# The opening of a two-block transformer kernel: products with the inverse root on GpSimd, pieces of three weight slabs on ScalarE, paired squares

## The chip, the cores and the metric

The kernel runs on one core of one Trainium2 chip. The time is the device time of one execution in microseconds: 2210.19 us before, the median of three runs (2209.67 to 2212.11).

## What is computed

Two transformer blocks on 512 tokens of width 1024, in float32. The first has a modulation (adaLN) from a vector c; the change lies in its first lines:

```
mod = silu(c) @ ada_w + ada_b
sh1, sc1, gt1, sh2, sc2, gt2 = split(mod, 6)
h = rms_norm(x, norm1_gain) * (1.0 + sc1) + sh1
z = h @ w_in            # then latent attention, sparse attention, output projections,
                        # a gated MLP; the second block has two layers more
```

where `rms_norm(x, g) = x * rsqrt(mean(x * x) + 1e-6) * g`.

## The kernel before

All activations lie feature-major: `xT` is 128 partitions x 8 chunks (k) x 512 tokens. For accuracy each operand of a matrix product is split into a high part (rounded) and a low part (the rest); every product of the input stage is three TensorE instructions (`three`, lines 1130 to 1132): high by high, high by low, low by high. Weights stream from memory as slabs of 128 x 2048 into the two buffers of `raw`; of each slab `w_hi` and `w_lo` are made, by GpSimd in this stage. A slab of `w_in` holds four chunks k; two slabs make one chunk of 512 output columns. Processing of one k is 12 TensorE instructions (four blocks of tokens by three). The first two slabs processed are numbers 2 and 3 of the stream (called first and second here), then numbers 0 and 1 (third and fourth), then the rest in order. The buffer of a slab is reloaded when its split is done (`slab_split`, waited for by SyncE, SP), and its `w_hi` and `w_lo` are free when TensorE is through with it (`slab_used`).

Each engine has one program in order; they meet through semaphores. The opening runs as follows.

- SP issues the transfers in the order c (`crow`), `xT`, `consts` (among them the mean matrix and the identity), `cols` (gains and biases as columns), then the rows of `ada_w` in pairs (shift and scale of chunk k; rows 0 to 2, a slab, 3 and 4, a slab, 5 to 7), then small tables.
- ScalarE computes silu(c) twice (L2154, L2155), waits for the whole of x, loads the table of Sqrt, and squares the eight chunks of x into `t1` (`norm`, L1991).
- TensorE multiplies each square by the mean matrix (L1144; a float32 product of 512 columns is two passes), then runs 16 products with the identity (L1149) that serve nothing but to keep it busy. ScalarE takes the root (L1998), VectorE the reciprocal into PSUM (L2969).
- VectorE computes the modulation: for each k two products of a row of `ada_w` with silu(c) summed into `mod` (`first_shift`, `first_scale`, L2924). ScalarE folds in biases and gain (`first_mod`, L2162, L2164).
- Then for each k: VectorE forms x times scale times inverse root in PSUM bank 5 (`first_part`, L2952), ScalarE adds the shift and rounds to `h_hi` (L2173), VectorE makes `h_lo` (`first_low`, L2957). With one bank for the part, the next part waits for the low half. Rows for k + 1 are computed between part and low half.
- GpSimd splits the first two slabs in pieces of 512 (`split_first`, high L789, low L786), later slabs whole or in pieces (`split`, L668, L672).
- TensorE waits for piece and low half of each k (`first_ready`) and starts; after the first two slabs (into banks 0 to 3) `chunk` does the next ones, a slab at a time, with other work between (`compress_turn`, 16 transposes, L1661, between the third and the fourth slab).

Of the kernel before, what the change touches and what calls it, by code (L numbers as in the profile page):

```python
# [28 lines left out]
KD = D_MODEL // P  # L29
# [192 lines left out]
def build(nc, xT_d, slabs_d, ada_d, c_d, cols_d, rows_d, consts_d, strips_d, pos_d, cpos_d,  # L222
# [5 lines left out]
    with ctx:  # L228
# [186 lines left out]
        const_loaded, crow_loaded, x_loaded = sem("const_loaded"), sem("crow_loaded"), sem("x_loaded")  # L415
        rest_loaded = sem("rest_loaded")
        ada_first_loaded = [sem(f"ada_first_loaded{q}") for q in range(KD)]
        mod_summed, mod_ready, inv_kept = sem("mod_summed"), sem("mod_ready"), sem("inv_kept")
# [144 lines left out]
        def _(sp):  # L563
# [18 lines left out]
            sp.dma_start(xT[:], xT_d).then_inc(x_loaded, 16)  # L582
            for dst, src in ((consts[:], consts_d), (cols[:], cols_d)):
                sp.dma_start(dst, src).then_inc(const_loaded, 16)
# [67 lines left out]
        def _(pool):  # L652
# [127 lines left out]
            def split_first(n):  # L780
                pool.wait_ge(slab_loaded[n], 16)
                cuts = [slice(a, a + PIECE) for a in range(0, SLAB, PIECE)]

                def low(j):
                    pool.wait_ge(piece_hi, 4 * n + j + 1)
                    nc.gpsimd.tensor_tensor(w_lo[:, n, cuts[j]], raw[:, n, cuts[j]], w_hi[:, n, cuts[j]].bitcast(f32),  # L786
                                            ALU.subtract).then_inc(piece_split, 1)
                for j in range(4):
                    nc.gpsimd.tensor_tensor(w_hi[:, n, cuts[j]], raw[:, n, cuts[j]], zero[:, 0:PIECE], ALU.add  # L789
                                            ).then_inc(piece_hi, 1)  # L790
                    if j > 0:
                        low(j - 1)
                pool.drain().then_inc(hi_done, 1)
                low(3)
                pool.drain().then_inc(slab_split, 1)
# [51 lines left out]
            split_first(0)  # L847
            split_first(1)
            with pool.Fori(1, N_IN // 2) as i:
                for s in (0, 1):  # L850
                    split(s, 2 * i + s, i, piece=PIECE)
# [273 lines left out]
        def _(pe):  # L1125
# [8 lines left out]
            def norm(t, residual=True, warm=16):  # L1134


                ks = (3, 5, 6, 7) if residual else range(KD)
                for k in ks:
                    if residual and k < 6:
                        pe.wait_ge(pair_ready, at_.pairs + 1)  # L1140
                        at_.pairs += 1
                    else:
                        pe.wait_ge(sq_ready, KD * at_.norms + k + 1)
                    last = nc.tensor.matmul(PS[:, 0, :], mean_w, t[:, k, :], start=not residual and k == 0,  # L1144
# [42 lines left out]
            def chunk(bank0, ready=None, banks_ready=None, between=None, n=512):  # L1187

                for s in (0, 1):
                    pe.wait_ge(slab_split, at_.slab + 1)  # L1190
                    slab_tokens(at_.slab % 2, h_hi, h_lo, 4 * s, 4, n, bank0, 1, s == 0, s == 1, ready,
# [461 lines left out]
            pe.wait_ge(const_loaded, 16 * 2)  # L1653
            norm(t1, residual=False)
# [137 lines left out]
            chunk(4, between=during_q)  # L1792
# [188 lines left out]
        def _(act):  # L1981
# [3 lines left out]
            def norm(t, hi, shift=None, residual=True):  # L1985

                A(small[:, 8:9], eps_c, ACT.Sqrt)
                for k in range(KD):
                    if residual:
                        act.wait_ge(x_ready, at_.x + k + 1)  # L1990
                    A(PS[:, k, :] if residual and k in (0, 2, 4) else t[:, k, :], xT[:, k, :], ACT.Square  # L1991
# [165 lines left out]
            act.wait_ge(x_loaded, 16)  # L2157
            norm(t1, None, residual=False)

            def first_mod(k):  # L2160
# [3 lines left out]
                A(mod[:, k:k + 1], mod[:, k:k + 1], ACT.Identity, bias=col("ada_b", k)).then_inc(mod_ready, 1)  # L2164

            for k in (0, 1, 2):
                first_mod(k)
            for k in range(KD):
                if k > 2:
                    first_mod(k)  # L2170
                act.wait_ge(part_ready, k + 1)
                act.drain()
                A(h_hi[:, k, :], PS[:, 5, :], ACT.Identity, bias=mod[:, k:k + 1]).then_inc(part_hi, 1)  # L2173
                if k == 2:
                    A(inv_rms[:], PS[:, 4, :], ACT.Copy).then_inc(inv_kept, 1)
# [477 lines left out]
        def _(dve):  # L2653
# [294 lines left out]
            def first_part(k):  # L2948
                dve.wait_ge(mod_ready, k + 1)
                if k > 0:  # L2950
                    dve.wait_ge(part_low, k)
                V.scalar_tensor_tensor(out=PS[:, 5, :], in0=xT[:, k, :], scalar=sc1[:, k:k + 1], in1=PS[:, 4, :],  # L2952
                                       op0=ALU.mult, op1=ALU.mult).then_inc(part_ready, 1)

            def first_low(k):
                dve.wait_ge(part_hi, k + 1)
                V.scalar_tensor_tensor(out=h_lo[:, k, :], in0=PS[:, 5, :], scalar=sh1[:, k:k + 1],  # L2957
                                       in1=h_hi[:, k, :].bitcast(f32), op0=ALU.add, op1=ALU.subtract
                                       ).then_inc(part_low, 1)

            dve.wait_ge(x_loaded, 16)
            dve.wait_ge(const_loaded, 16 * 2)
            then(V.scalar_tensor_tensor(out=norm1_b, in0=col("ada_b", KD, KD), scalar=1.0, in1=col("norm1", 0, KD),
                                        op0=ALU.add, op1=ALU.mult))
            for k in (0, 1, 2):
                first_shift(k)
                first_scale(k)
            dve.wait_ge(root_ready, 1)
            then(V.reciprocal(PS[:, 4, :], PS[:, 1, :]))  # L2969
            for k in (0, 1, 2):  # L2970
                first_part(k)
                if k == 1:
                    first_shift(3)
                elif k == 2:
                    first_scale(3)
                first_low(k)
            for k in range(3, KD):
                first_part(k)
                if k + 1 < KD:
# [730 lines left out]
```

## Time and profile before

| | |
|---|---|
| median of three runs | 2210.19 us |
| the profiled execution | 2209.41 us |
| span of that execution, first to last instruction | 2207.6 us |
| TensorE busy | 2147.7 us, 97% |
| VectorE busy | 1504.0 us, 68% |
| GpSimd busy | 1195.1 us, 54% |
| ScalarE busy | 954.0 us, 43% |

The chain that ended last lies on TensorE for 85% of the span and on VectorE for 8%. Shares of the span are means over stages with different limits. In the first of 40 slices of the span (55 us each) TensorE is busy for six tenths, in all the later ones but the last for nine tenths or more, so the opening is read by itself.

### The profile page before, as it was taken

What the parts mean: (1) busy time and instruction counts of PE and PEld (TensorE: products, weight loads), DVE (VectorE), ACT (ScalarE), POOL (GpSimd) and SP (SyncE); (2) the same over time, 40 slices, a digit from 0 to 9 for tenths busy, and PEclk for the clock granted to TensorE, in tenths of its full rate; (3) what the DMA queues carried; (4) which work ended last, traced back from release to release, by engine and by line L of the source; (5) the groups of instructions that cost most, each with busy time, mean ns of one, the idle gap of its engine ahead of it and who ended that gap; (6) DMA issues with size and microseconds to landing.
All of it is one profiled execution on the core that took longest, in us unless ns stands there. A gap on an engine that the chain in (4) does not pass through costs nothing.

```text
span 2207.6 us, 33182 instructions
## 1 busy us (share of the span) xinstructions
PE 2147.7 (97%) x12377; PEld 1839.9 (83%) x12377; DVE 1504.0 (68%) x2242; ACT 954.0 (43%) x1905; POOL 1195.1 (54%) x594
## 2 busy tenths in 40 slices
PE   6999999999999999999999999999999999999997
PEld 4788888877899988897887898888897887889886
DVE  6834777554666692897746776677996727767676
ACT  3264663011556610644743555412545725555312
POOL 4747403776477677745016644577653037544675
PEclk9999999999999999999999999999999999999999
DMA  8422202522133333232002222322221012223221
GB/s 318 156 72 83 68 30 94 189 80 96 58 116 115 113 140 134 77 115 77 1 13 84 96 96 95 115 96 85 106 85 69 1 35 82 88 103 115 96 96 57
DMA packets 32776, 206.78 MB, mean 94 GB/s; under 512 B 4080, under 2 KB 4336, under 8 KB 11632
## 3 DMA queue, kind: packets, MB, share of 16 engines
q1 hardware_dynamic: 32192, 200.27, 25.2%
q10 hardware_dynamic: 432, 4.46, 0.5%
q8 instruction: 99, 1.62, 0.3%
q14 instruction: 53, 0.43, 0.1%
HBM read 202.61 MB, written 2.10 MB: 93 GB/s over the span
## 4 chain that ended last, share of the span: by engine, by line
PE 85%; DVE 8%; issue 2%; ACT 2%; DVEq 1%; DMA 1%; POOL 1%; POOLq 0%; SPq 0%; ACTq 0%
PE PS L1130 18%; PE PS L1132 18%; PE PS L1131 18%; PE PS L1626 4%; PE PS L1615 4%; PE PS L1385 3%; PE PS L1387 3%; PE PS L1386 3%; PE PS L1461 2%; PE PS L1463 2%; PE PS L1462 2%; PE PS L1640 2%; PE PS L1260 1%; PE PS L1263 1%; PE PS L1262 1%
## 5 line engine op out<-in xcount | busy, mean ns | idle before, releaser
L668 POOL TENSOR_TENSOR w_hi<-raw,zero_c 128x512 fp32r<-128x512 f32 (+1 forms) x135 | 281.6, 2104 | 545.0 <-PE PS L1132 543.7
L672 POOL TENSOR_TENSOR w_lo<-raw,w_hi 128x512 fp32r<-128x512 f32 (+1 forms) x135 | 365.0, 2722 | 5.8
L1130 PE MATMUL PS<-b_hi,w_hi 128*128 128x512 f32 x512 | 203.1, 397 | 1.0 <-POOL w_lo L891 1.0
L1132 PE MATMUL PS<-b_hi,w_lo 128*128 128x512 f32 x512 | 203.0, 396 | 0.0
L1131 PE MATMUL PS<-b_lo,w_hi 128*128 128x512 f32 x512 | 203.0, 396 | 0.0
L3376 DVE TENSOR_TENSOR b_lo<-a_all,b_hi 128x512 fp32r<-128x512 f32 x44 | 162.6, 3734 | 49.3 <-ACT b_hi L2511 49.3
L1130 PE MATMUL PS<-f_hi,w_hi 128*128 128x512 f32 x448 | 177.6, 396 | 0.7 <-DVE f_lo L2668 0.7
L1132 PE MATMUL PS<-f_hi,w_lo 128*128 128x512 f32 x448 | 177.6, 396 | 0.0
L1131 PE MATMUL PS<-f_lo,w_hi 128*128 128x512 f32 x448 | 177.6, 396 | 0.0
L691 POOL TENSOR_TENSOR w_lo<-raw,w_hi 128x512 fp32r<-128x512 f32 x48 | 71.1, 1481 | 92.7 <-ACT w_hi L2503 92.7
L1130 PEld LDWEIGHTS PS<-b_hi,w_hi 128*128 128x128 f32 x512 | 96.4, 188 | 24.7 <-POOL w_lo L891 1.2
L1132 PEld LDWEIGHTS PS<-b_hi,w_lo 128*128 128x128 f32 x512 | 96.4, 188 | 23.5
L1131 PEld LDWEIGHTS PS<-b_lo,w_hi 128*128 128x128 f32 x512 | 96.4, 188 | 23.5
L1626 PEld LDWEIGHTS PS<-z,ring 128*128 128x128 f32 x640 | 87.0, 191 | 25.7 <-issue 12.2
L1132 PEld LDWEIGHTS PS<-f_hi,w_lo 128*128 128x128 f32 x448 | 84.4, 188 | 20.5
L1130 PEld LDWEIGHTS PS<-f_hi,w_hi 128*128 128x128 f32 x448 | 84.4, 188 | 20.1 <-issue 1.0
L1131 PEld LDWEIGHTS PS<-f_lo,w_hi 128*128 128x128 f32 x448 | 84.4, 188 | 19.1
L2511 ACT ACTIVATE b_hi<-a_all 128x512 fp32r<-128x512 f32 x44 | 25.3, 623 | 171.4 <-PE PS L1132 171.4
L680 POOL TENSOR_TENSOR w_lo<-raw,w_hi 128x2048 fp32r<-128x2048 f32 (+1 forms) x18 | 59.1, 3295 | 62.3 <-ACT w_hi L2363 62.3
L776 POOL TENSOR_TENSOR w_lo<-raw,w_hi 128x512 fp32r<-128x512 f32 x54 | 70.8, 1311 | 38.0 <-ACT w_hi L2401 38.0
L3338 DVE SCALAR_TENSOR_TENSOR aux<-PS,cols,aux 128x511 f32<-128x511 f32 (+1 forms) x112 | 81.0, 741 | 14.7 <-ACT aux L2483 13.5
L1626 PE MATMUL PS<-z,ring 128*128 128x64 f32 x640 | 85.3, 266 | 1.3 <-ACT ring L2145 1.3
(600 smaller groups left out, 6890.1 us busy)
## 6 DMA issues: line engine op xcount, KB each, us to landing
raw<-slabs_dram SPq DMA_DIRECT2D x161, 1024.0 KB, 4.8
aux<-ada_dram SPq DMA_DIRECT2D x18, 512.0 KB, 5.5
ada_first<-ada_dram SPq DMA_DIRECT2D x11, 512.0 KB, 14.2
cmpw<-cmpw_dram ACTq DMA_DIRECT2D x2, 2048.0 KB, 12.0
ada_late<-ada_dram SPq DMA_DIRECT2D x8, 512.0 KB, 3.4
ada_last<-ada_dram SPq DMA_DIRECT2D x8, 512.0 KB, 6.1
xT<-xT_dram SPq DMA_DIRECT2D x1, 2048.0 KB, 9.2
out_dram<-t SPq DMA_DIRECT2D x4, 512.0 KB, 3.2
```

Of the source, the lines that this page charges most:

```text
L668: high = nc.gpsimd.tensor_tensor(w_hi[:, slot, c], raw[:, slot, c], zero[:, 0:c.stop - c.start], ALU.add)
L672: low = nc.gpsimd.tensor_tensor(w_lo[:, slot, c], raw[:, slot, c], w_hi[:, slot, c].bitcast(f32), ALU.subtract)
L691: return nc.gpsimd.tensor_tensor(pair_ring(w_lo, ct, n, what), pair_operand(ct, n, what), pair_ring(w_hi, ct, n, what).bitcast(f32), ALU.s ...
L776: nc.gpsimd.tensor_tensor(ring_slot(w_lo, j), operand(j), ring_slot(w_hi, j).bitcast(f32), ALU.subtract).then_inc(slab_split if name == "A ...
L1130: nc.tensor.matmul(out, a_hi_, b_hi_, start=start, stop=False)
L1131: nc.tensor.matmul(out, a_hi_, b_lo_, start=False, stop=False)
L1132: return nc.tensor.matmul(out, a_lo_, b_hi_, start=False, stop=stop)
L1385: nc.tensor.matmul(out, wh[:, k, :], xh, start=first, stop=False, skip_group_check=True)
L1615: last = nc.tensor.matmul(out, q, keys[:, 128 * lo:128 * (lo + nb)], start=True, stop=True)
L1626: last = nc.tensor.matmul(PS[:, 6 + m % O_BANKS, 64 * j:64 * j + 64], turned_slot(ring, v, 512)[:, 128 * b:128 * b + 128], jobs[m]["v"](lo ...
L3338: V.scalar_tensor_tensor(out=t[:, sh:], in0=src[:, 0:SEQ - sh], scalar=cols[:, w:w + 1], in1=t[:, sh:], op0=ALU.mult, op1=ALU.add)
L3376: V.tensor_tensor(b_lo[:, f, :], a_all[:, f, :], b_hi[:, f, :].bitcast(f32), ALU.subtract).then_inc(b_low_ready, 1)
```

## The change

x is loaded in two halves, each with its own semaphore, with the constants between them; the mean on TensorE waits for the constants only, and the columns are waited for together with the first modulation rows. ScalarE loads its table before it waits for x. VectorE adds the squares in pairs, so the mean is four products instead of eight, followed by 20 identity products instead of 16. The reciprocal goes straight into SBUF (`inv_rms`). GpSimd multiplies x by it, chunk by chunk, into `t1`, one chunk ahead. ScalarE makes `h_hi` from that with scale and shift, writes shift minus `h_hi` into PSUM (banks 4 and 5 in turn), and copies the pieces of the first three slabs into `w_hi`; GpSimd makes their `w_lo`. VectorE makes `h_lo` as product times scale plus what ScalarE left in PSUM. Rows 1 and 2 of the modulation come ahead of the first low half, rows 3 to 7 spread behind. The third slab is waited for by pieces on TensorE.

```diff
@@ -579,9 +579,11 @@
...
             sp.dma_start(crow[:], c_d.partition_broadcast(P)).then_inc(crow_loaded, 16)
-            sp.dma_start(xT[:], xT_d).then_inc(x_loaded, 16)
-            for dst, src in ((consts[:], consts_d), (cols[:], cols_d)):
-                sp.dma_start(dst, src).then_inc(const_loaded, 16)
+            for i in (0, 1):
+                sp.dma_start(xT[:, 4 * i:4 * i + 4, :], xT_d[:, 4 * i:4 * i + 4, :]).then_inc(x_loaded[i], 16)
+                if i == 0:
+                    sp.dma_start(consts[:], consts_d).then_inc(const_loaded, 16)
+            sp.dma_start(cols[:], cols_d).then_inc(ada_first_loaded[0], 16)
             for k in (0, 1, 2):
@@ -777,22 +779,24 @@
...
-            def split_first(n):
-                pool.wait_ge(slab_loaded[n], 16)
-                cuts = [slice(a, a + PIECE) for a in range(0, SLAB, PIECE)]
-
-                def low(j):
-                    pool.wait_ge(piece_hi, 4 * n + j + 1)
-                    nc.gpsimd.tensor_tensor(w_lo[:, n, cuts[j]], raw[:, n, cuts[j]], w_hi[:, n, cuts[j]].bitcast(f32),
+            def first_slabs():
+                def normed(k):
+                    nc.gpsimd.tensor_tensor(t1[:, k, :], xT[:, k, :], inv_rms[:], ALU.mult).then_inc(part_ready, 1)
+
+                pool.wait_ge(inv_kept, 1)
+                normed(0)
+                for k in range(KD + 4):
+                    if k + 1 < KD:
+                        normed(k + 1)
+                    n, c = k // 4 % 2, slice(PIECE * (k % 4), PIECE * (k % 4) + PIECE)
+                    if k >= KD:
+                        pool.wait_ge(slab_used, 1)
+                    pool.wait_ge(piece_hi, k + 1)
+                    nc.gpsimd.tensor_tensor(w_lo[:, n, c], raw[:, n, c], w_hi[:, n, c].bitcast(f32),
                                             ALU.subtract).then_inc(piece_split, 1)
-                for j in range(4):
-                    nc.gpsimd.tensor_tensor(w_hi[:, n, cuts[j]], raw[:, n, cuts[j]], zero[:, 0:PIECE], ALU.add
-                                            ).then_inc(piece_hi, 1)
-                    if j > 0:
-                        low(j - 1)
-                pool.drain().then_inc(hi_done, 1)
-                low(3)
-                pool.drain().then_inc(slab_split, 1)
+                    if k % 4 == 3:
+                        pool.drain().then_inc(hi_done, 1)
+                        pool.drain().then_inc(slab_split, 1)
@@ -844,9 +848,9 @@
...
             n_pieces = (N_IN + N_TAIL + N_QB + N_KVB) // 2
-            split_first(0)
-            split_first(1)
-            with pool.Fori(1, N_IN // 2) as i:
+            first_slabs()
+            split(1, 3, 1, piece=PIECE)
+            with pool.Fori(2, N_IN // 2) as i:
                 for s in (0, 1):
@@ -1134,14 +1138,14 @@
...
-                ks = (3, 5, 6, 7) if residual else range(KD)
+                ks = (3, 5, 6, 7) if residual else (1, 3, 5, 7)
                 for k in ks:
-                    if residual and k < 6:
+                    if not residual or k < 6:
                         pe.wait_ge(pair_ready, at_.pairs + 1)
...
                         pe.wait_ge(sq_ready, KD * at_.norms + k + 1)
-                    last = nc.tensor.matmul(PS[:, 0, :], mean_w, t[:, k, :], start=not residual and k == 0,
+                    last = nc.tensor.matmul(PS[:, 0, :], mean_w, t[:, k, :], start=not residual and k == ks[0],
                                             stop=k == ks[-1])
@@ -1187,8 +1191,9 @@
...
                 for s in (0, 1):
-                    pe.wait_ge(slab_split, at_.slab + 1)
-                    slab_tokens(at_.slab % 2, h_hi, h_lo, 4 * s, 4, n, bank0, 1, s == 0, s == 1, ready,
+                    if not ready or s:
+                        pe.wait_ge(slab_split, at_.slab + 1)
+                    slab_tokens(at_.slab % 2, h_hi, h_lo, 4 * s, 4, n, bank0, 1, s == 0, s == 1, None if s else ready,
                                 banks_ready if s == 0 else None,
@@ -1650,8 +1655,8 @@
...
             meet()
-            pe.wait_ge(const_loaded, 16 * 2)
-            norm(t1, residual=False)
+            pe.wait_ge(const_loaded, 16)
+            norm(t1, residual=False, warm=20)
@@ -1789,7 +1794,7 @@
...
             at_.slab += 2
-            chunk(4, between=during_q)
+            chunk(4, ready=lambda k: pe.wait_ge(piece_split, KD + k + 1), between=during_q)
             chunk(0, banks_ready=lambda tt: pe.wait_ge(cmp_dve if tt % 2 else cmp_act, tt // 2 + 1),
@@ -1988,6 +1993,8 @@
...
                         act.wait_ge(x_ready, at_.x + k + 1)
+                    else:
+                        act.wait_ge(x_loaded[k // 4], 16)
                     A(PS[:, k, :] if residual and k in (0, 2, 4) else t[:, k, :], xT[:, k, :], ACT.Square
@@ -2154,25 +2161,33 @@
...
             meet()
-            act.wait_ge(x_loaded, 16)
             norm(t1, None, residual=False)
...
                   bias=norm1_b[:, k:k + 1])
-                A(mod[:, k:k + 1], mod[:, k:k + 1], ACT.Identity, bias=col("ada_b", k)).then_inc(mod_ready, 1)
-
-            for k in (0, 1, 2):
+                A(mod[:, k:k + 1], mod[:, k:k + 1], ACT.Identity, bias=col("ada_b", k))
+
+            def piece_high(k):
+                n, c = k // 4, slice(PIECE * (k % 4), PIECE * (k % 4) + PIECE)
+                act.wait_ge(slab_loaded[n % 2], 16 * (n // 2) + 16)
+                A(w_hi[:, n % 2, c], raw[:, n % 2, c], ACT.Copy).then_inc(piece_hi, 1)
+
+            for k in range(KD):
                 first_mod(k)
-            for k in range(KD):
-                if k > 2:
-                    first_mod(k)
                 act.wait_ge(part_ready, k + 1)
                 act.drain()
-                A(h_hi[:, k, :], PS[:, 5, :], ACT.Identity, bias=mod[:, k:k + 1]).then_inc(part_hi, 1)
-                if k == 2:
-                    A(inv_rms[:], PS[:, 4, :], ACT.Copy).then_inc(inv_kept, 1)
+                A(h_hi[:, k, :], t1[:, k, :], ACT.Identity, scale=mod[:, KD + k:KD + k + 1], bias=mod[:, k:k + 1])
+                act.drain()
+                if k >= 2:
+                    act.wait_ge(part_low, k - 1)
+                A(PS[:, 4 + k % 2, :], h_hi[:, k, :].bitcast(f32), ACT.Identity, scale=-1.0, bias=mod[:, k:k + 1]
+                  ).then_inc(part_hi, 1)
+                piece_high(k)
+            act.wait_ge(slab_used, 1)
+            for k in range(KD, KD + 4):
+                piece_high(k)
             at_.part += KD
@@ -2945,40 +2960,26 @@
...
-            def first_part(k):
-                dve.wait_ge(mod_ready, k + 1)
-                if k > 0:
-                    dve.wait_ge(part_low, k)
-                V.scalar_tensor_tensor(out=PS[:, 5, :], in0=xT[:, k, :], scalar=sc1[:, k:k + 1], in1=PS[:, 4, :],
-                                       op0=ALU.mult, op1=ALU.mult).then_inc(part_ready, 1)
-
             def first_low(k):
                 dve.wait_ge(part_hi, k + 1)
-                V.scalar_tensor_tensor(out=h_lo[:, k, :], in0=PS[:, 5, :], scalar=sh1[:, k:k + 1],
-                                       in1=h_hi[:, k, :].bitcast(f32), op0=ALU.add, op1=ALU.subtract
-                                       ).then_inc(part_low, 1)
-
-            dve.wait_ge(x_loaded, 16)
-            dve.wait_ge(const_loaded, 16 * 2)
+                V.scalar_tensor_tensor(out=h_lo[:, k, :], in0=t1[:, k, :], scalar=sc1[:, k:k + 1],
+                                       in1=PS[:, 4 + k % 2, :], op0=ALU.mult, op1=ALU.add).then_inc(part_low, 1)
+
+            for k in range(0, KD, 2):
+                dve.wait_ge(sq_ready, k + 2)
+                V.tensor_tensor(t1[:, k + 1, :], t1[:, k, :], t1[:, k + 1, :], ALU.add).then_inc(pair_ready, 1)
+            dve.wait_ge(ada_first_loaded[0], 48)
             then(V.scalar_tensor_tensor(out=norm1_b, in0=col("ada_b", KD, KD), scalar=1.0, in1=col("norm1", 0, KD),
                                         op0=ALU.add, op1=ALU.mult))
-            for k in (0, 1, 2):
-                first_shift(k)
-                first_scale(k)
+            first_shift(0)
+            first_scale(0)
             dve.wait_ge(root_ready, 1)
-            then(V.reciprocal(PS[:, 4, :], PS[:, 1, :]))
-            for k in (0, 1, 2):
-                first_part(k)
-                if k == 1:
-                    first_shift(3)
-                elif k == 2:
-                    first_scale(3)
-                first_low(k)
-            for k in range(3, KD):
-                first_part(k)
-                if k + 1 < KD:
-                    first_shift(k + 1)
-                    first_scale(k + 1)
+            V.reciprocal(inv_rms[:], PS[:, 1, :]).then_inc(inv_kept, 1)
+            ahead = {0: (1, 2), 1: (3,), 3: (4,), 4: (5,), 5: (6,), 6: (7,)}
+            for k in range(KD):
+                for row_ in ahead.get(k, ()):
+                    first_shift(row_)
+                    first_scale(row_)
                 first_low(k)
```

## Rows read from the trace of the kernel before

**Rows 1.** Busy time by stage: stretch, length, busy of five engines, clock, DMA.
```profile
46.74:51.19 4.45, 3.05 (x13) 2.19 (x13) 3.82 (x7) 1.26 (x3) 4.45 (x4) 1.00 0.01 2
51.19:56.85 5.66, 5.66 (x24) 4.59 (x25) 4.25 (x20) 0.69 (x1) 0.53 (x1) 1.00 0.74 269
75.00:150.00 75.00, 75.00 (x362) 57.54 (x361) 50.88 (x63) 29.02 (x46) 43.95 (x35) 1.00 0.20 71
```

**Rows 2.** Chain that ended last, in order of time: start us, us, what.
```profile
1.20 9.21 DMA xT<-xT_dram
10.50 1.28 ACT L1987
...
12.66 9.85 PE PS L1144 x16
22.54 0.67 ACT PS L1998
23.23 3.37 DVE PS L2969
...
42.69 0.76 DVE PS L2952
43.45 1.12 DVEq L2946
...
45.85 0.76 DVE h_lo L2957
...
51.19 0.47 PE PS L1130
```

**Rows 3.** Timeline of the opening: start us, us, instruction, idle before and its releaser.
```profile
5.50 1.03 ACT L2154 ACTIVATE PS<-crow 128x1024 f32<-128x1024 f32 x1 [3.48 <-DMA crow<-c_dram]
6.46 1.04 ACT L2155 ACTIVATE crow<-crow 128x1024 f32<-128x1024 f32 x1
...
11.91 4.25 ACT L1991 ACTIVATE t<-xT 128x512 f32<-128x512 f32 x8
...
17.07 0.34 PEld L1144 LDWEIGHTS PS<-t,consts 128*128 128x128 f32 x1 [0.52 <-issue]
...
21.05 1.06 SPq L566 DMA_DIRECT2D ada_spare<-ada_dram  x1
...
22.34 7.07 PE L1149 MATMUL PS<-consts 128*128 128x256 f32 x32
...
37.74 0.39 ACT L2162 ACTIVATE mod<-mod,small,cols 128x1 f32<-128x1 f32 x1 [1.56 <-DVEq L2946]
```

**Rows 4.** DMA issues of the first 120 us: count, size, us to landing.
```profile
consts<-consts_dram SPq DMA_DIRECT2D x1, 460.0 KB, 9.6
```

**Rows 5.** The tile `ada_spare` (the last modulation rows), first 60 us.
```profile
DMA to landing us min/median/max: 16.6/18.2/19.0
```

**Rows 6.** Groups by line and shape, whole span: busy us, mean ns; idle before.
```profile
L811 POOL TENSOR_TENSOR m_rope<-q_m,trig 128x512 f32<-128x512 f32 x1 | 1.3, 1295 | 0.1
L786 POOL TENSOR_TENSOR w_lo<-raw,w_hi 128x512 fp32r<-128x512 f32 x8 | 10.3, 1285 | 0.4 <-issue 0.4
L2678 DVE RECIPROCAL t<-t 128x512 f32<-128x512 f32 x3 | 10.1, 3353 | 11.7 <-ACT t L2356 8.3 <-ACT t L1998 3.4
L2008 ACT ACTIVATE g_hi<-t,mod 128x512 fp32r<-128x512 f32 x8 | 5.7, 722 | 6.7 <-DVE t L2685 6.7
L2401 ACT ACTIVATE w_hi<-raw 128x512 fp32r<-128x512 f32 x54 | 34.0, 629 | 32.7 <-DMA raw<-slabs_dram 23.0 <-PE PS L1132 6.1 <-PE PS L1387 3.6
```

**Rows 7.** Timeline of GpSimd and VectorE behind the opening.
```profile
57.16 4.05 POOL L668 TENSOR_TENSOR w_hi<-raw,zero_c 128x512 fp32r<-128x512 f32 x4 [5.44 <-PE PS L1132]
61.29 5.03 POOL L672 TENSOR_TENSOR w_lo<-raw,w_hi 128x512 fp32r<-128x512 f32 x4
...
92.44 8.31 POOL L668 TENSOR_TENSOR w_hi<-raw,zero_c 128x512 fp32r<-128x512 f32 x4 [0.87 <-PE PS L1132]
93.16 2.47 DVE L2838 TENSOR_TENSOR z<-z,stats 128x2048 f32<-128x2048 f32 x1
```

More of the change, by code:

```diff
@@ L412, in build @@
         lam_c = small[:, 2:3]
-        const_loaded, crow_loaded, x_loaded = sem("const_loaded"), sem("crow_loaded"), sem("x_loaded")
+        const_loaded, crow_loaded, x_loaded = sem("const_loaded"), sem("crow_loaded"), [sem(f"x_loaded{i}") for i in (0, 1)]
         rest_loaded = sem("rest_loaded")
         ada_first_loaded = [sem(f"ada_first_loaded{q}") for q in range(KD)]
-        mod_summed, mod_ready, inv_kept = sem("mod_summed"), sem("mod_ready"), sem("inv_kept")
+        mod_summed, inv_kept = sem("mod_summed"), sem("inv_kept")
         piece_hi, piece_split = sem("piece_hi"), sem("piece_split")
@@ L3172, in _ @@
             meet()
-            dve.wait_ge(inv_kept, 1)
             scaled(t2, g_hi, g_lo, inv_rms[:], sc1, sh1)
```

## The prediction

> **What bounds the kernel now.** I read the busy time of the engines by stages first, then the chain of waits through the first 57 us, then the timeline of that stretch, and last the groups of instructions for prices. By stages TensorE is busy in every microsecond from 51.19 to 56.85 us and from 75 to 150, but between 46.74 and 51.19 in only 3.05 of 4.45 us [rows 1]. So TensorE is the limit once the opening is over, and a change in the opening is worth as many microseconds as it brings forward the moment from which TensorE no longer waits.
>
> The chain says what sets that moment [rows 2]. x lands at 10.41 us (1.20 + 9.21). ScalarE then loads its table (10.50, 1.28 us), the squares follow, the sixteen passes of the mean run from 12.66 to 22.51, the root takes 0.67, VectorE's reciprocal runs from 23.23 to 26.60. From there the chain stays on VectorE: part (0.76), two rows of the modulation with a drain (43.45 to 45.85, 2.40), low half (0.76), again and again, 4.0 us and more for one k. TensorE needs less: 24 products, two k, took 5.66 us, so 2.83 each [rows 1]. It therefore waits about a microsecond per k, and starts the seventh (k = 6) at 51.19 [rows 2]; from there it runs without a gap, and the first two slabs end at 56.85, with GpSimd, which waited for them, starting at 57.16 [rows 7]. Eight k are 22.6 us of work; 56.85 is the time to beat.
>
> **The change part by part.**
>
> *Constants and x.* x comes in two halves with the constants between, the columns after. The vector c has landed at 5.44, when ScalarE starts on it [rows 3], and x 5.0 us behind it. Taking the queue to deliver in order, the first half lands midway, at 7.9, the 460 KB of constants [rows 4], under a quarter of x, about 1.1 us later at 9.0, the second half at 11.5. The bytes ahead of the modulation's rows stay the same; the one more issue costs SP some 0.4 us, behind transfers that are queued anyway.
>
> *Squares.* ScalarE's table load no longer stands behind the wait for x. It follows the Silu that ends at 7.50 (6.46 + 1.04), so the first square starts at 7.55 + 1.41 = 8.96; the 1.41 is 11.91 less 10.50. Eight squares took 4.25, 0.53 each [rows 3]. Two are done at 10.1, four at 11.1; the second half runs from 11.55 to 13.8.
>
> *Pairs and mean.* VectorE adds four pairs at no more than the 0.76 of a part; it was idle until its first row. The first is done at 10.9, the last at 14.6. The mean is eight passes now, from 10.95. Before, the weight loads came 0.86 apart at 17.07 (0.34 + 0.52 idle [rows 3]); at that pace sixteen passes would take 13.8, and they took 9.85, so the later ones went at half of it, 0.43. Eight passes take 3.4 at the one pace and 6.9 at the other. I take the slow one nearly to the end, 17.7, since it still held at 17.07 last time. That is 4.8 before 22.51. Bounds of the mean's end: 16.5, if the last pass follows the last pair at once, and 17.9.
>
> *Root and reciprocal.* VectorE's modulation of row 0 takes 2.4 us from its landing near 15, so it is over before the root. Root 0.67 to 18.45, reciprocal into SBUF 3.35 [rows 6] to 21.9, against 26.60.
>
> *x times the root on GpSimd.* VectorE loses the part; GpSimd gains eight products and loses eight copies to the high half. The trace has the operation on that engine: a product of two SBUF tiles of 512 took 1.30, its low halves in the opening 1.29 [rows 6]. Bounds: 1.01, the copies (4.05 for four), and 2.08, the four that took 8.31 while VectorE worked on SBUF tiles alone [rows 7]. VectorE's rows and low halves here each read one SBUF tile and one of PSUM, as those beside the 1.29 did, so I take 1.30; GpSimd has 2.6 per k. The Trainium skill (GPSIMD Engine Reference, Engine selection) puts elementwise products on VectorE, GpSimd being about twice as slow for two inputs. The trace agrees, 1.30 against 0.76; by that rule alone the move loses 0.54 per k, by the rows it wins, because VectorE was the pace and GpSimd had room.
>
> *ScalarE per k.* Shift and scale 0.39 and no more than that again [rows 3], high half 0.72 [rows 6], the new negated copy to PSUM 0.67 as the root that writes there, the piece of the slab 0.63 [rows 6]: 2.7, and about 3.0 with the handovers. Bounds 2.7 and 3.6 (two drains at 0.2, a dearer high half with scale and bias).
>
> *VectorE per k.* Two rows and the drain 2.40, low half 0.76: 3.2 against 4.0. Rows 1 and 2 stand ahead of the first low half: reciprocal 21.9, rows to 27.0, low half 0 to 27.75, row 3 to 30.2, low half 1 to 30.95. No row is due at k = 2. Then every 3.2: low halves 3 to 6 at 34.9, 38.1, 41.3, 44.5. The last waits for ScalarE (row 7 done at 43.7, then the two small ones, high half and copy, 2.1, and 0.76): 46.6. Row 7 is wanted at 41.2; its last issue at 21.05 [rows 3] with the longest landing, 19.0 [rows 5], is 40.05.
>
> *TensorE.* Twenty identity products in place of sixteen: 32 instructions took 7.07 [rows 3], so 40 take 8.8, from 17.7 to 26.5, and it waits 1.3 us for k = 0 at 27.85. k = 1 starts at 31.05. From there every input is early (k = 5: 41.3 against 42.4; k = 6: 44.5 against 45.2; the slab's last low piece, GpSimd, 47.8 against 48.0), so seven k at 2.83 end at 50.9. **That is 5.95 us before 56.85.**
>
> *The third slab by pieces.* ScalarE copies its four pieces from 46.5 to 48.9, GpSimd's low pieces come at 49.2, 50.5, 51.8, 53.1; TensorE takes one per 2.83 from 50.9 and never waits. Late next is the fourth slab: its buffer comes free only with the last low piece, 47.9, it lands some 5 us later, at 53, or up to 56 if the compression weights, which ScalarE issues at 48.9, share the queue. GpSimd needs 9.2 for it (57.16 to 66.32 [rows 7]), so 62.3 to 65.2, and TensorE asks for it at 50.9 + 11.3 + 1.9 (the transposes) = 64.1. Loss 0 to 1.1; I take none. From the fifth slab on GpSimd waits for TensorE as before, and the lead stays.
>
> **Sum.** The profiled execution took 2209.41 for a span of 2207.6; less 5.9 that is 2203.5. The median, 2210.19, lies 0.8 above it, so I forecast 2204.3.
>
> **The rivals.**
>
> *Given back in part.* The hand-to-hand chain of ScalarE, GpSimd and VectorE has margins of only 0.2 to 1.1 us. At a pace of 3.4 per k from 27.85 TensorE ends at 27.85 + 7 x 3.4 + 2.83 = 54.5, a gain of 2.4; the fourth slab late by 1 to 2 us in its place leaves 4 to 5. For it: ScalarE takes on two more instructions per k. Against it: VectorE's 3.2 is measured work, and a k without a row gives slack. About 2207.2.
>
> *Slower: GpSimd becomes the bound.* Its sixteen instructions from 21.9 on now stand in front of TensorE. At a price p TensorE ends at 21.9 + 16p + 2.83, which passes 56.85 from p = 2.0. At the 2.08 of [rows 7] it ends at 58.0, 1.2 late; at 2.4 it is 63.1, 6.3 late, 2216.5. For it: GpSimd does slow down in company. Against it: 1.29 beside the very same rows. The Trainium skill (GPSIMD Engine Reference, Specifications) names VectorE instructions with two SBUF inputs as those that contend with GpSimd. By that rule only the four pair additions count, when GpSimd stands still; the trace agrees, 1.29 beside one SBUF input and 2.08 beside two.
>
> *No change at the end.* The opening gains 6 us and something that doesn't follow TensorE takes it back: 2209.5 to 2210.5. For it: 2150 us of program follow, and I have priced 15. Against it: loads are issued when slabs are split or used, so they move along, and TensorE is full from 75 to 150 us.
>
> **How the numbers follow.** Forecast 0.66 (its own range 2202.5 to 2205.8, from the mean's end at 16.5 or 17.9, and a microsecond lost to the fourth slab), given back in part 0.20, no change 0.08, slower 0.06. The range goes to 2201.8 below, for a pace that doubles early, and to 2208.3, which takes in most of the second case and leaves out the last two. A measurement of this kernel tells 0.2% (4.4 us) from no change: faster by that are the forecast and a little of the second case, 0.69; within it 0.26; slower 0.05.
>
> **What would show it.** In the new trace: first square near 9.0; mean over at 17.7 with eight passes; reciprocal ending at 21.9; products on GpSimd at 1.3; TensorE's first slab product near 27.9 and no wait from about 31; the two slabs over at 50.9; the fourth slab's low half before 64. A mean that ends after 19, a GpSimd product near 2, low halves more than 3.3 apart, or a wait of TensorE of over 2 us between 51 and 75 would make the prediction wrong.

## The result, and the profile after

The kernel after takes 2214.14 us, the median of 20 runs (2211.14 to 2215.78), beside 2210.84 for the kernel before, the median of 20 runs (2208.20 to 2213.63). The ratio is 1.0016, with a 95% interval of 1.0010 to 1.0022. It is 3.3 us slower. The forecast was 2204.3 in a range of 2201.8 to 2208.3, so both the sign and the range were wrong. The profiled execution after took 2213.46, for a span of 2211.3.

The head of the page of the kernel after, to be held against the busy times of before:

```profile
span 2211.3 us, 33193 instructions
...
PE 2150.0 (97%) x12377; PEld 1845.3 (83%) x12377; DVE 1501.1 (68%) x2238; ACT 966.5 (44%) x1924; POOL 1197.4 (54%) x590
```

TensorE is busy for 2.3 us more than before; where the time went has to be read from the opening. The timeline of the kernel after (start, length, instruction; in brackets the idle time before it and what ended it) gives the opening that [rows 2, 3] gave of before:

```profile
9.00 2.17 ACT L1998 ACTIVATE t<-xT 128x512 f32<-128x512 f32 x4
...
11.11 5.18 PE L1148 MATMUL PS<-t,consts 128*128 128x512 f32 x8 [11.11 <-DVE t L2970]
...
17.50 3.36 DVE L2977 RECIPROCAL inv_rms<-PS 128x512 f32<-128x512 f32 x1
...
21.01 2.51 POOL L784 TENSOR_TENSOR t<-xT,inv_rms 128x512 f32<-128x512 f32 x2 [20.17 <-DVE inv_rms L2977]
...
26.61 0.47 PE L1134 MATMUL PS<-w_hi,h_hi 128*128 128x512 f32 x1 [1.69 <-DVE h_lo L2965]
...
43.63 0.69 ACT L2185 ACTIVATE PS<-h_hi,mod 128x512 f32<-128x512 f32 x1
43.85 0.86 ACTq L2193 DMA_DIRECT2D cmpw<-cmpw_dram  x2
44.26 2.70 ACT L2175 ACTIVATE w_hi<-raw 128x512 fp32r<-128x512 f32 x5
49.65 1.88 ACT L2197 ACTIVATE z<-PS 128x2048 f32<-128x2048 f32 x1 [2.69 <-PE PS L1136]
...
62.70 5.58 POOL L674 TENSOR_TENSOR w_lo<-raw,w_hi 128x512 fp32r<-128x512 f32 x4
...
81.57 1.88 ACT L2197 ACTIVATE z<-PS 128x2048 f32<-128x2048 f32 x1 [18.81 <-PE PS L1136]
```

The same two takes of ScalarE (`z` from PSUM, after two slabs and after four) in the kernel before, with what ScalarE and its queue did ahead of them:

```profile
52.00 0.69 ACT L2173 ACTIVATE h_hi<-PS,mod 128x512 fp32r<-128x512 f32 x1 [1.20 <-DVE PS L2952]
52.01 0.86 ACTq L2178 DMA_DIRECT2D cmpw<-cmpw_dram  x2
57.05 1.88 ACT L2182 ACTIVATE z<-PS 128x2048 f32<-128x2048 f32 x1 [4.36 <-PE PS L1132]
...
81.19 1.88 ACT L2182 ACTIVATE z<-PS 128x2048 f32<-128x2048 f32 x1 [11.03 <-PE PS L1132]
```

The opening brought all that it was to bring and more. The first take came at 49.65 instead of 57.05, a lead of 7.40 us (6.4 against two other profiles of the old opening, see r2 and c1 below). The second came at 81.57 instead of 81.19. So 7.8 us were lost between the two takes. The chain of waits of the kernel after (start, length, what) shows where:

```profile
46.46 12.07 DMA raw<-slabs_dram
...
58.59 2.04 POOL w_hi L670 x2
```

This is the fourth slab. It was issued at 46.46 and took 12.07 us to land; in the kernel before it took 4.7. The waits of the kernel after in the first 170 us (engine, line, released by whom: total, times, longest):

```profile
POOL w_hi L670 <- DMA raw<-slabs_dram: 6.9, 1, 6.9
...
PE PS L1134 <- POOL w_lo L674: 5.8, 1, 5.8
...
PE PS L1134 <- DVE h_lo L2965: 1.7, 1, 1.7
```

and TensorE's first product of that slab in the timeline:

```profile
68.34 0.80 PE L1134 MATMUL PS<-w_hi,h_hi 128*128 128x512 f32 x1 [5.78 <-POOL w_lo L674]
```

GpSimd stood 6.9 us for the slab, split it until 68.3 (62.70 + 5.58), and TensorE stood 5.8 us for that. About half a microsecond of it is a slower split: 5.58 for the low half, where the kernel before took 5.03 [rows 7]. Then the clock came on top. By windows (stretch, length, busy time of PE, PEld, DVE, ACT and POOL, granted clock, DMA share, GB/s):

```profile
62.00:64.00 2.00, 0.56 (x6) 0.33 (x3) 1.73 (x3) 0.60 (x1) 1.92 (x3) 1.00 0.00 0
...
66.00:68.00 2.00, 0.00 (x0) 0.00 (x0) 2.00 (x2) 0.00 (x0) 2.00 (x2) 0.50 0.00 0
...
70.00:72.00 2.00, 2.00 (x6) 1.52 (x6) 2.00 (x2) 0.00 (x0) 2.00 (x3) 0.50 0.82 336
72.00:74.00 2.00, 2.00 (x10) 1.65 (x9) 1.83 (x3) 0.00 (x0) 1.92 (x2) 0.96 0.31 131
```

TensorE idled from 62.5 and the granted clock fell to 0.50, the 1.2 GHz level. Work came back at 68.3, the clock only at about 72.1 (a mean of 0.96 in 72 to 74): six products in 70 to 72, ten in 72 to 74. These 3.8 us at half speed cost 1.9. Wait and clock together are 5.8 + 1.9 = 7.7 of the 7.8.

Why was the slab late? The 4 MB of compression weights (two halves, `cmpw`) had been issued by ScalarE at 43.85, 2.6 us ahead of it. In the kernel before TensorE's first product of them is at 92.3, so they are in no hurry. There the fourth slab was issued at 41.32, and it had landed at 46.1, eleven microseconds before GpSimd came to it at 57.16 [rows 7]; the weights went out at 52.01. The change issues the slab five microseconds later and the weights eight earlier, so the two pass each other. The issue in the timeline of before, and the landings of the slabs issued there from 40 to 75 us:

```profile
41.32 0.33 SPq L570 DMA_DIRECT2D raw<-slabs_dram  x1
...
DMA to landing us min/median/max: 4.7/5.0/7.8
```

The 7.8 is the fifth slab, issued at 51.90 beside the weights; nothing waited for it.

The DMA queues of the kernel after show what the weights did to the slab (packets, MB, share of the 16 engines; q10 carries ScalarE's issues, q1 SP's). The first line is the stretch from 46.46 to 49.8, the other two that from 50 to 57:

```profile
q10 hardware_dynamic: 87, 1.43, 99.6%
...
q10 hardware_dynamic: 140, 2.03, 67.8%
q1 hardware_dynamic: 130, 1.00, 33.7%
```

For 3.3 us not one packet of the slab moved; where it is alone, in e5 below, its first packet starts 1.0 us after the issue. From then on the two queues moved nearly as many packets each, but those of the weights hold about twice the bytes, so the slab had a third of the traffic.

### The profile page after: what moved, and what is told of

Its sections match the earlier page's. It is cut to its first block, busy times and chain, and to the rows that moved or that the text cites. A ratio compares the mean times of both kernels' runs of the same rounds, so it can differ in the third digit from the quotient of the medians.

```text
span 2211.3 us, 33193 instructions
## 1 busy us (share of the span) xinstructions
PE 2150.0 (97%) x12377; PEld 1845.3 (83%) x12377; DVE 1501.1 (68%) x2238; ACT 966.5 (44%) x1924; POOL 1197.4 (54%) x590
## 4 chain that ended last, share of the span: by engine, by line
PE 81%; DVE 8%; DMA 2%; issue 2%; ACT 2%; DVEq 2%; POOL 2%; POOLq 1%; SPq 0%; ACTq 0%
PE PS L1134 17%; PE PS L1136 17%; PE PS L1135 17%; PE PS L1631 4%; PE PS L1620 4%; PE PS L1390 3%; PE PS L1392 3%; PE PS L1391 3%; PE PS L1645 2%; PE PS L1466 2%; PE PS L1468 2%; PE PS L1467 2%; DMA raw<-slabs_dram 2%; DVE PS L3464 1%; POOL w_lo L674 1%
## 5 line engine op out<-in xcount | busy, mean ns | idle before, releaser
L670 POOL TENSOR_TENSOR w_hi<-raw,zero_c 128x512 fp32r<-128x512 f32 (+1 forms) x131 | 275.8, 2123 | 543.8 <-PE PS L1136 536.8
```

The source lines that it names most:

```text
L670: high = nc.gpsimd.tensor_tensor(w_hi[:, slot, c], raw[:, slot, c], zero[:, 0:c.stop - c.start], ALU.add)
```

## The experiments

A reading used throughout is the lag: the start of one and the same ScalarE instruction in a run's trace less its start in the profiled execution of before, so that a negative number is a lead. Positions are those in the trace of before; from 160 on each is the median of a stretch.

| run | at 57 | at 81 | 160 to 225 | 245 to 300 | 750 to 800 | end |
|---|---|---|---|---|---|---|
| after | -7.40 | +0.38 | +0.41 | +1.43 | +3.10 | +3.77 |
| e1 weights later | -6.31 | -6.29 | -5.20 | -4.17 | -2.47 | -0.38 |
| e5 weights later still | -7.43 | -7.41 | -7.38 | -7.40 | -7.40 | -7.29 |
| q1 weights in order | -7.58 | -7.58 | -6.92 | -6.92 | -5.20 | -3.40 |
| w1 no idle TensorE | -6.26 | -1.02 | -1.00 | -0.98 | +0.77 | +2.52 |
| p1 e5 without pairs | -3.50 | -3.50 | -3.50 | -2.48 | +1.17 | +1.12 |
| b1 before, slab late | -0.85 | +8.89 | +8.91 | +8.90 | +10.68 | +10.60 |
| c1 before, weights later | -0.97 | -0.97 | -0.94 | +0.09 | +1.88 | +1.59 |
| r2 before, again | -1.05 | -1.03 | -1.02 | -1.04 | +0.79 | +0.56 |

**The weights later.** The change as it stands, with the issue of the weights behind ScalarE's two copies into the stage:

```diff
             at_.part += KD
-            for kv in (0, 1):
-                act.dma_start(cmpw[:, kv, :, :], cmpw_d[:, kv, :, :]).then_inc(cmpw_loaded[kv], 16)
...
             A(c_stage[:, :, :, 1, :], staged, ACT.Copy).then_inc(stage_ready, 1)
+            for kv in (0, 1):
+                act.dma_start(cmpw[:, kv, :, :], cmpw_d[:, kv, :, :]).then_inc(cmpw_loaded[kv], 16)
```

> The changed kernel with one move: ScalarE issues the two transfers of the compression weights (4 MB) not behind its last piece (43.85 us) but behind its copies for the transposes, near 54 us. Theory 1 (the gain is lost because the fourth slab's transfer, issued at 46.46, shares the queues with those 4 MB and lands after 12.07 us): the slab lands near 51.5, its low half is ready near 61, TensorE has no wait of over 0.5 us between 51 and 75, ends the fourth slab near 74 where the kernel before ended it at 81.2, and the lead of about 7 us stays to the end: 2203.5 (2202 to 2205.5). Theory 2 (GpSimd would be late anyway, slowed by VectorE's small instructions beside it): low half not before 64, 2207 to 2210. Theory 3 (later stages take the lead back whatever the opening does): lead of 7 at 80 us, but 2209 or more at the end.

Measured: 2206.85 (2203.07 to 2210.03), ratio 0.9983 [0.9974, 0.9992]. One move of one issue turns slower into faster, though by less than expected. Timeline of this run:

```profile
52.71 1.06 ACT L2210 ACTIVATE aux<-z 128x1024 f32<-128x1024 f32 x1
52.76 0.85 ACTq L2213 DMA_DIRECT2D cmpw<-cmpw_dram  x2
53.68 1.05 ACT L2211 ACTIVATE aux<-z 128x1024 f32<-128x1024 f32 x1
...
57.26 5.05 POOL L674 TENSOR_TENSOR w_lo<-raw,w_hi 128x512 fp32r<-128x512 f32 x4
65.22 4.50 POOL L670 TENSOR_TENSOR w_hi<-raw,zero_c 128x512 fp32r<-128x512 f32 x4 [2.91 <-DMA raw<-slabs_dram]
```

The fourth slab is split at 62.3 and TensorE doesn't wait. But the issue went out at 52.76, ahead of the second copy (53.68) that it follows in the program, and the fifth slab, issued at 53.10, 0.3 us behind it, is now the one that takes 12.0 us: GpSimd waits 2.9, TensorE 0.8, and a microsecond of the lead is gone by 99. The stall had been handed on by one slab, smaller.

**The control.** The same move in the kernel before (same edit).

> Control: the kernel before with the same move of the compression weights. Theory 1: nothing waits for them there and the fourth slab had landed long ahead of them, so the time is that of the kernel before within 1 us (2210 to 2212). Theory 2 and 3 expect the same; a gain of over 2 us would mean that the move helps by itself, and the first experiment could not be read as it is.

Measured: 2211.22 (2209.03 to 2212.59), ratio 1.0002 [0.9993, 1.0011]. So the place of the weights is worth nothing in the old opening, where TensorE waits for no slab that comes behind them.

**The late slab by itself.** The kernel before, where SP issues the fourth slab only once the first half of the weights has landed:

```diff
                 sp.wait_ge(slab_split, s + 1)
+                if s:
+                    sp.wait_ge(cmpw_loaded[0], 16)
                 load_slab(s, s)
```

> The kernel before with one wait added on SP: the transfer of the fourth slab is issued only when the first half of the compression weights has landed, some 58 to 60 us in place of 41.32. It puts the late slab alone into the old opening. Theory 1: it lands near 65, the low half is ready near 75, TensorE, which asks at 70, waits 5 us or more, its granted clock falls to 0.50 for a few us, and the time is 6 to 9 us above the kernel before (2217 to 2220). Theory 3 (later stages set the time): less than 3 us above it.

Measured: 2219.98 (2219.25 to 2221.81), ratio 1.0045 [1.0031, 1.0059]. Its longest wait of TensorE among the waits of 50 to 100 us (total, times, longest):

```profile
PE PS L1132 <- POOL w_lo L674: 7.0, 1, 7.0
```

The same stretch by busy time and clock, columns as in the windows above:

```profile
50.00:100.00 50.00, 42.73 (x180) 34.45 (x181) 32.86 (x58) 14.74 (x15) 31.53 (x26) 0.90 0.43 168
```

TensorE stood 7.0 us, the granted clock fell to a mean of 0.90, and the lag went from -0.85 to +8.89, 9.7 in all. The medians differ by 8.9. A late fourth slab alone, in a kernel with the old opening, costs its wait and 2.7 us more, and none of it comes back. The clock accounts for the 2.7: it stands at 0.50 when work comes back at 76.1 and returns at about 81.6 (0.59 in 80 to 82, 1.00 in 82 to 84), and 5.5 us at half speed cost 2.8.

**The wait without the idle.** The change, with the 16 transposes that stand ahead of the fourth slab's products done four times over, so that TensorE works while it waits:

```diff
                 for n in range(4):
-                    for tt in range(TT):
+                    for tt in list(range(TT)) * 4:
```

> The changed kernel with the 16 transposes between the third and the fourth slab done four times over (same result), so that TensorE is at work during 5 of the 5.8 us that it waited for the fourth slab. Theory 1 with the clock: in the changed kernel TensorE started that slab at 68.3 with a granted clock of 0.50 that rose only near 72; kept busy it starts at the same moment at full clock and gains some 1.9 us: 2212.2 (2211 to 2213). If the clock costs nothing there: 2214, as the changed kernel.

Measured: 2211.34 (2209.75 to 2214.33), ratio 1.0002 [0.9993, 1.0011]; the median is 2.8 under that of the change. Its window, and from its timeline TensorE's first product of the fourth slab and ScalarE's second take:

```profile
50.00:100.00 50.00, 50.00 (x251) 39.92 (x250) 34.87 (x47) 14.54 (x15) 39.54 (x31) 1.00 0.38 149
...
68.69 0.48 PE L1134 MATMUL PS<-w_hi,h_hi 128*128 128x512 f32 x1
...
80.17 1.88 ACT L2197 ACTIVATE z<-PS 128x2048 f32<-128x2048 f32 x1 [12.34 <-PE PS L1136]
```

The clock stays at 1.00, with 48 transposes of no use. What they can't remove is the wait for the data, which they fill to 68.7. From the slab's first product to the second take 11.48 us pass, in the change 13.23 (68.34 to 81.57): 1.75 given back, close to the 1.9 that the clock was said to cost. Between the two takes 5.24 us are lost instead of 7.78, but part of that difference is only that this run's first take was 1.1 us later, for a reason of its own (a granted clock of 0.75 in 25 to 30 us), so that there was less to wait for. The 2.8 of the medians is more than the clock explains; the rest is not shown.

**The weights behind everything.** The change, with the issue behind ScalarE's two copies of `c_kT`, which wait for TensorE's transposes:

```diff
                 A(c_kT[:, n, :], PS[:, n, :], ACT.Copy).then_inc(cmp_act, 1)
+            for kv in (0, 1):
+                act.dma_start(cmpw[:, kv, :, :], cmpw_d[:, kv, :, :]).then_inc(cmpw_loaded[kv], 16)
```

> The changed kernel with the compression weights issued later still, behind ScalarE's copies of the transposes (about 66 us). In the first experiment the fifth slab took the fourth one's place: issued at 52.8 beside the weights (52.76), landed at 65.2, and 1.06 us of lead was lost by 94 us. Theory 1: now the fourth and the fifth slab both land 5 us after their issue, TensorE waits for no slab, the lead of 6.3 us at 81 is still there at 99 and at 165, and the time is about 1 us under the first experiment's 2206.9: 2205.8 (2204 to 2207). Theory 2 (GpSimd and VectorE, which slow each other here, hold the lead below that): lead falls between 81 and 99 all the same, 2207 or more.

Measured: 2205.15 (2202.76 to 2209.09), ratio 0.9978 [0.9968, 0.9987]. It beats both kernels, that before by 6.1 us and the change by 9.0 us of medians. Its timeline:

```profile
51.99 4.07 POOL L670 TENSOR_TENSOR w_hi<-raw,zero_c 128x512 fp32r<-128x512 f32 x4 [0.36 <-issue]
...
70.90 0.38 ACTq L2219 DMA_DIRECT2D cmpw<-cmpw_dram  x1
...
73.78 1.88 ACT L2195 ACTIVATE z<-PS 128x2048 f32<-128x2048 f32 x1 [1.46 <-PE PS L1136]
```

The landings of the tile of slabs issued from 40 to 75 us:

```profile
DMA to landing us min/median/max: 4.7/4.8/5.4
```

Every one of them lands in 4.7 to 5.4 us, TensorE waits for nothing from 30 to 110, and the lead of 7.4 stands at 57, at 81 and at the end. The weights come in good time even so: TensorE's first product of them starts at 84.9, which is 92.3 less 7.4.

**The weights in order.** The change, with the same 4 MB issued 2.8 us later than there, by SP right behind the fourth slab on its own queue:

```diff
                 load_slab(s, s)
+            sp.wait_ge(mod_summed, KD)
+            for kv in (0, 1):
+                sp.dma_start(cmpw[:, kv, :, :], cmpw_d[:, kv, :, :]).then_inc(cmpw_loaded[kv], 16)
```

> The changed kernel with the same 4 MB issued by SP right behind the fourth slab, on the same queue, in place of ScalarE's queue. Theory 1 holds that sharing by two queues is what stretched the fourth slab to 12.07 us. Here the 4 MB are issued at nearly the same time as in the changed kernel but behind the slab in one queue: the fourth slab lands some 5 us after its issue (51.5), the fifth, queued behind the 4 MB, near 64; TensorE has no wait over 1 us, 2205 to 2207.5. If the mere presence of the 4 MB in flight stretches the slab, it lands near 58 again and the time is 2213 to 2215.

Measured: 2206.33 (2204.20 to 2208.49), ratio 0.9978 [0.9969, 0.9987]. Its timeline on SP's queue and GpSimd:

```profile
46.28 0.33 SPq L570 DMA_DIRECT2D raw<-slabs_dram  x1
46.65 0.91 SPq L623 DMA_DIRECT2D cmpw<-cmpw_dram  x2
51.84 22.56 SPq L570 DMA_DIRECT2D raw<-slabs_dram  x3
51.85 4.07 POOL L673 TENSOR_TENSOR w_hi<-raw,zero_c 128x512 fp32r<-128x512 f32 x4 [0.36 <-issue]
...
63.49 4.49 POOL L673 TENSOR_TENSOR w_hi<-raw,zero_c 128x512 fp32r<-128x512 f32 x4 [2.45 <-DMA raw<-slabs_dram]
```

The slab issued 0.4 us ahead of the 4 MB is there when GpSimd is free at 51.85. The next, issued 5.2 us behind them, lands after 11.5, which costs TensorE a wait of 0.4 and 0.7 of the lead. So in one queue weights behind a slab don't delay it, and weights ahead of it do. On two queues the order protects less: the fifth slab of the kernel before went out 0.1 us ahead of the weights and took 7.8.

**The pairs by themselves.** The best version without the paired squares: sixteen passes again, and 16 identity products.

```diff
-                ks = (3, 5, 6, 7) if residual else (1, 3, 5, 7)
+                ks = (3, 5, 6, 7) if residual else range(KD)
...
-            for k in range(0, KD, 2):
-                dve.wait_ge(sq_ready, k + 2)
-                V.tensor_tensor(t1[:, k + 1, :], t1[:, k, :], t1[:, k + 1, :], ALU.add).then_inc(pair_ready, 1)
```

> The kernel of the first run of this group with the squares unpaired again (sixteen passes of the mean, no additions on VectorE, 16 identity products). It measures that part. The mean starts near 9.7 and ends near 19.3 where the changed kernel ended it at 16.3, so everything up to the third slab moves by 3 us: lead near 3.5 at 81 us and 2209 (2207.5 to 2210.5). If the pairs were worth nothing: the time of that first run, 2205.8.

Measured: 2209.23 (2202.34 to 2211.29), ratio 0.9985 [0.9976, 0.9994]. Its timeline:

```profile
9.76 9.93 PE L1148 MATMUL PS<-t,consts 128*128 128x512 f32 x16 [9.76 <-ACT t L1998]
...
20.42 3.36 DVE L2974 RECIPROCAL inv_rms<-PS 128x512 f32<-128x512 f32 x1 [2.93 <-ACT PS L2005]
...
53.55 1.89 ACT L2195 ACTIVATE z<-PS 128x2048 f32<-128x2048 f32 x1 [3.68 <-PE PS L1136]
```

and by window, columns as above:

```profile
30.00:32.00 2.00, 2.00 (x6) 1.52 (x5) 1.87 (x5) 1.86 (x5) 1.85 (x3) 0.50 1.04 414
```

The take at 53.55 instead of 49.62: the pairs are worth 3.9 of the 7.4, the rest of the opening 3.5. Of the 3.9 the later mean is 2.9 (first slab product at 29.53 instead of 26.59); the other microsecond is the clock, which stood at 0.50 in 30 to 32 behind a wait of 2.9, where e5 waited 1.2 and had 1.00. The medians say 4.1 for the pairs, but the eleven runs here spread over 9 us, so they say it loosely.

**Before, again.** The kernel before unchanged, for its trace alone.

> The kernel before, unchanged, for a second profile: how far two executions of one program lie apart in the stages behind the opening. The trace of before took 1366 products in the stretch 600 to 760 us where four other kernels took 1350, the control with the same stages among them. If that is chance of the execution, this profile shows 1350 too and is 1 to 2 us later at 760; if it belongs to the program, 1366.

Measured: 2209.96. Two windows of the first profiled execution of before:

```profile
230.00:235.00 5.00, 5.00 (x25) 5.00 (x24) 3.04 (x8) 2.56 (x9) 4.85 (x5) 0.50 0.00 0
...
600.00:760.00 160.00, 160.00 (x1366) 160.00 (x1365) 98.57 (x152) 94.86 (x187) 110.65 (x81) 1.00 0.31 109
```

The same two of this execution:

```profile
230.00:235.00 5.00, 4.24 (x37) 4.01 (x35) 4.32 (x16) 2.58 (x10) 4.79 (x4) 1.00 0.00 0
...
600.00:760.00 160.00, 160.00 (x1351) 160.00 (x1350) 98.27 (x152) 94.63 (x185) 110.27 (x80) 1.00 0.30 106
```

One program, twice: once with the clock at 0.50 in 230 to 235, once at 1.00; once 1366 products in 160 us without a gap at full clock, once 1351, and 15 products at 160 / 1366 are 1.8 us. The table has these 1.8: the lag of this run goes from -1.04 to +0.79 between 245 to 300 and 750 to 800. The clock in 230 to 235 left no trace in it (-1.02 before, -1.04 behind). So most of the later drift in the table is no trace of the change: against its own first profile before drifts +1.6 from 165 us to the end, and its control +2.5; the change drifts +3.4. The profiled execution of before also had its opening 1.0 us later than r2 and c1.

## Why the prediction was wrong

**The opening** was forecast by its steps and held. First square 8.96, measured 9.00. Mean over at 17.7, measured 16.3: the eight passes took 5.18, between the 3.4 and the 6.9 of the two paces, and in e1 they took 6.65, so this term moves by over a microsecond from run to run. The reciprocal was to end at 21.9 and ended at 20.9. One step failed at a small price: VectorE's row 0 was to be over before the root, but ended at 17.39, so the reciprocal waited half a microsecond. GpSimd's product, the disputed price, is 1.27 to 1.31 against 1.30. First slab product 26.61 against 27.85, behind a wait of 1.7 (1.3 forecast), and behind it TensorE waits for nothing until the fourth slab, as forecast. The lead is 7.40 where 5.95 was forecast; 1.24 of the difference is there at the first product, and most of that is the mean, which was taken too slow. Two slips of arithmetic are in the working: rows 1 and 2 end at 21.9 + 4.8 = 26.7, not at 27.0, and the terms named for the forecast's own range give 2203.1 (1.2 less) to 2205.5 (0.2 and 1.0 more), not 2202.5 to 2205.8. Neither matters for what follows.

**The step that failed** is in the paragraph on the third slab by pieces: "the compression weights, which ScalarE issues at 48.9", a landing "at 53, or up to 56", "Loss 0 to 1.1; I take none". The weights went out at 43.85, five microseconds early and ahead of the fourth slab instead of behind it; the slab landed at 58.52, and the loss was 7.8. Three things were wrong there.

First, the time of the issue. I dated it by the end of the last piece that ScalarE copies. The issue waits only until the instructions ahead of it have been handed to the engine: it stands at 43.85 while ScalarE is at the copy of 43.63 and five pieces still follow until 46.96, 3.1 us later. The other 1.9 of the five microseconds are the opening, whose last piece was to end at 48.9. The trace of before shows it too, the issue at 52.01 with the instruction ahead of it just begun at 52.00, and the prediction passed over it. The Trainium skill (Perfetto Trace Analysis, DVE / Act Engine Instruction) says that the sequencer goes on to the next instruction once one is pushed into the engine's wait queue. The trace agrees: the issue runs ahead of five activations.

Second, the price of being second. I let the slab share and gave it three more microseconds. It stood 3.3 us before its first packet moved and then had a third of the bytes: 12.07 in all, 12.0 for the slab of e1, against 4.7 to 5.4 in e5. Third, that TensorE's idle time has a price beyond itself: 5.8 us of wait cost 7.7, b1's 7.0 cost 9.7, and p1's 2.9 was followed by another microsecond.

"Given back in part" had the right place, the fourth slab, with a size of 1 to 2 us. "Slower" had the wrong engine: GpSimd's products were never the bound. That its prices, 1.2 to 6.3 us late, enclose the 3.3 measured is luck. "No change at the end" had the wrong cause too: where no slab is late, in e5, the lead of 7.4 is still there at the end. What I had named as a sign, "a wait of TensorE of over 2 us between 51 and 75", is what came. The version in which only that step is mended comes near the forecast: 2205.15 against 2204.3, and 6.1 us gained where 5.9 were forecast. Part of that nearness is luck: the mean was taken 1.4 us too slow, and the profile that the forecast was worked out from had its opening a microsecond later than r2 and c1.

**Do the books close?** Against r2 and c1, whose openings agree, the change stands at about +1.4 at 81 us and +2.7 at the end (3.77 less 1.1, the mean of 0.56 and 1.59); the medians say 3.3, with 2.2 to 4.9 by the interval. The column's end is not quite the span's: c1 and q1 lose another 1.2 us at their last instruction, and by spans the change stands at +2.1. For e5 the ends give -8.4, and its profiled execution was the fastest of its eleven, 2.4 under their median; that leaves -6.0, and the medians say -6.1. What makes one execution hold 1335, 1351 or 1366 products in the same 160 us (p1, r2, e5) at a granted clock of 1.00 is open; nothing here was aimed at it. So is the clock in 225 to 240 us, whose mean is 1.00 in e5 and r2, 0.95 in b1, and 0.66 to 0.84 in the other seven. The four with the lowest means, 0.66 to 0.76 (the change, c1, p1, e1), lose a microsecond of lag there, the other six nothing.

## What to carry to other kernels

When an edit moves a stage, list every DMA that the moved engines issue and hold each against the loads that it can now overtake; an issue that nobody waits for is as able to spoil the lead as one that is late, and a queue of its own doesn't keep it out of the way. Date an issue by when its engine's queue reaches it, not by the end of the arithmetic written ahead of it, and if it must come late, put it behind a wait that is itself late. A stall of TensorE is to be priced with what the clock takes after it: 1.0 to 2.7 us behind the three stalls of 2.9 to 7.0 us here.

## What the runs showed that was not expected

- A DMA issue on ScalarE's queue overtakes queued activations: 43.85 with five still to start in the change, 52.76 with one still to start in e1.
- 1 MB issued 0.3 to 2.6 us behind 4 MB on the other queue lands in 11.9 to 12.1 us (the change, e1, w1, and r2, where nothing waits for it); 5.2 us behind them on the same queue in 11.5. The slab is not held until all 4 MB are through, but the turns are uneven: in 50 to 57 us of the change its queue moved 130 packets against 140, and 1.00 MB against 2.03, with the 3.3 us before its first packet on top. The Trainium skill (DMA: Bandwidth & Descriptors, Queues, rings and completion order) has each DMA engine take turns between queues by packets. The trace agrees in the packets.
- The same program holds 1351 or 1366 products in the same 160 us, at full clock and without a gap, a difference of 1.8 us that the lags of the two profiles of the kernel before bear out.
